# The SSD mixer's exit: gating, turning and projecting the scan's output in parts, with D x moved into the scan

## The reference, cut to what matters

```
    def finish(y_f, y_b, xs, z):
        bb, L = xs.shape[:2]
        y = y_f + flip(y_b) + D_skip[:, None] * xs
        y = y.reshape(bb, L, D_INNER).astype(z.dtype)
        return rmsnorm(y * jax.nn.silu(z), norm_w) @ out_w
```

```
        x = x + g1l * o_lat
            ctx = ctx + g1c * o_ctx
```

## Time and profile before

| | us |
|---|---|
| median of 3 runs | 4000.08 |
| lowest and highest | 3996.6, 4001.8 |
| the profiled execution's own time | 4008.97 |
| its span | 4007.2 |

### The profile page before, as it was taken

The page is one execution under the profiler, slowest core; times in us unless marked ns, Lnnn a source line. Parts: engine busy times, 40 slices in busy tenths (PEclk is TensorE's granted clock), DMA queues, the critical chain, the costliest instruction groups (busy, mean ns, idle before and its releaser), DMA issues. The chain is left out here.

```text
span 4007.2 us, 44450 instructions
## 1 busy us (share of the span) xinstructions
PE 3488.9 (87%) x17221; PEld 2512.8 (63%) x17225; DVE 2320.7 (58%) x2842; ACT 1673.2 (42%) x2522; POOL 1467.4 (37%) x706
## 2 busy tenths in 40 slices
PE   5999989967959999959897899997797997659997
PEld 3778878953447666646566455554685645538876
DVE  1037666772159999963663999997118842233311
ACT  3112123432028777751452677775323321342212
POOL 3323322340046666632004466664323201214432
PEclk9989998988969999979998899999878999779999
DMA  6324444432069999944104899997122223113130
GB/s 223 134 83 144 170 162 129 130 137 105 0 254 369 385 388 384 385 165 147 64 1 152 316 377 379 379 378 272 48 69 71 90 85 121 53 69 105 63 136 27
DMA packets 307214, 716.30 MB, mean 179 GB/s; under 512 B 16240, under 2 KB 63180, under 8 KB 303932
## 3 DMA queue, kind: packets, MB, share of 16 engines
q1 hardware_dynamic: 300176, 692.27, 46.6%
q0 software_dynamic: 6144, 20.98, 2.5%
q10 hardware_dynamic: 684, 0.21, 0.0%
HBM read 659.88 MB, written 53.54 MB: 178 GB/s over the span
## 5 line engine op out<-in xcount | busy, mean ns | idle before, releaser
L133 POOL TENSOR_TENSOR weights_low<-ring,weights_high 128x1024 fp32r<-128x1024 f32 (+2 forms) x210 | 497.0, 2372 | 1148.9 <-ACT weights_high L126 1141.4
L579 PE MATMUL ps<-h_parts,weights_high 128*128 128x512 f32 (+2 forms) x2528 | 744.4, 380 | 39.5 <-POOL weights_low L133 33.0
L579 PEld LDWEIGHTS ps<-h_parts,weights_high 128*128 128x128 f32 (+1 forms) x2528 | 465.0, 192 | 150.4 <-POOL weights_low L133 36.4
L579 PE MATMUL ps<-h_parts,weights_low 128*128 128x512 f32 (+2 forms) x1264 | 476.7, 377 | 0.0
L1741 DVE TENSOR_TENSOR more_low<-area,more_high 128x1024 fp32r<-128x1024 f32 x192 | 330.6, 1760 | 0.0
L1708 ACT ACTIVATE weights_high<-ring 128x1024 fp32r<-128x1024 f32 x256 | 271.2, 1061 | 137.2 <-PE ps L1641 92.6
L126 ACT ACTIVATE weights_high<-ring 128x1024 fp32r<-128x1024 f32 (+1 forms) x158 | 161.4, 1039 | 355.7 <-PE ps L579 231.7
L1708 ACT ACTIVATE more_high<-area 128x1024 fp32r<-128x1024 f32 x256 | 271.7, 1062 | 86.0 <-PE ps L1641 85.9
L1741 DVE TENSOR_TENSOR weights_low<-ring,weights_high 128x1024 fp32r<-128x1024 f32 x192 | 300.3, 1617 | 2.7 <-ACT weights_high L1708 2.7
L1612 POOL TENSOR_TENSOR more_low<-area,more_high 128x1024 fp32r<-128x1024 f32 x64 | 243.1, 3798 | 110.8 <-ACT more_high L1708 110.8
L579 PE MATMUL ps<-weights_high,h_parts 128*128 128x512 f32 (+2 forms) x832 | 256.0, 387 | 20.4 <-POOL weights_low L133 20.4
(11 more groups left out here) (433 smaller groups left out, 7244.4 us busy)
## 6 DMA issues: line engine op xcount, KB each, us to landing
ring<-in_moe_w SPq DMA_DIRECT2D x96, 2048.0 KB, 10.8
area<-in_moe_w SPq DMA_DIRECT2D x96, 2048.0 KB, 10.5
ring<-in_ada_w SPq DMA_DIRECT2D x24, 2048.0 KB, 8.0
ring<-in_ssd_in_w SPq DMA_DIRECT2D x12, 2048.0 KB, 11.1
ring<-in_w_in SPq DMA_DIRECT2D x11, 2048.0 KB, 8.0
ring<-in_w_ffn_in SPq DMA_DIRECT2D x10, 2048.0 KB, 7.7
area<-x_dram SPq DMA_DIRECT2D x18, 1024.0 KB, 5.0
ring<-in_ssd_out_w SPq DMA_DIRECT2D x4, 2048.0 KB, 7.9
```

The source lines that it names most:

```text
L133: pool.tensor_tensor(lo, views[k][:, ks, cols], hi, ALU.subtract).then_inc(self.low_p, 1)
L579: mm = pe.matmul(out, a, b, start=start and n == 0, stop=stop and n == 2)
```

## The change

- In the scan, GpSimd multiplies x by D for each head group of the first direction (into dx) and adds it to t.y when VectorE has written that. SyncE loads D ahead of the first chunk, and a chunk's buffers are free only when these additions are done too (skip_s).
- gate_turn takes the place of norm_turn. Tile by tile, from the last to the first, VectorE multiplies y by z, TensorE turns the product at once in four banks of four blocks, ScalarE squares and sums and writes each bank's high part, VectorE the low part. The root and its reciprocal are made once for all tiles at the end. Neither the root nor the norm weight is applied here.
- ssd_out takes the place of project_add. ScalarE and VectorE make the weights' high and low parts with the norm weight as a scale (one number for each row of out_w), TensorE makes three fp32r products, and VectorE takes the sums out of PSUM with the reciprocal root and the gate row in one instruction, and adds to X. GpSimd has no part in either stage.

```diff
--- before.py
+++ after.py
@@ -1005,6 +1005,8 @@
         state = st.sb("state", [P, DI])
         ex = st.sb("segment_exp", [P, 2, W4])
         acT, sel = st.sbr("acum_turned_parts", [P, NT, P]), st.sbr("pick_head_rows", [P, 2 * H])
+        dsk, dx = st.sb("d_skip", [P, H]), st.sb("d_times_x", [P, W])
+        d_in, skip_s = st.sem("d_in"), st.sem("skip_added")
         y1 = st.sb("y_off", [P, 2, W])
         y2 = st.sb("y_sum", [P, 2, W])
         acT_s, acT_h, acT_l = st.sem("acum_turned"), st.sem("acum_turned_high"), st.sem("acum_turned_low")
@@ -1022,11 +1024,13 @@
         @block.sync
         def _(sp):
             env.ring_.load_to(sp, len(env.ring_.ends) + SLOTS)
+            sp.dma_start(dsk, env.ins["ssd_D"].rearrange("a h -> (a h)").partition_broadcast(P)).then_inc(d_in, 16)
             v = lambda x, m: x[:, m % 2, :].rearrange("p (g c) -> p g c", g=G)
             for m, (d, i, c) in enumerate(steps):
                 if m >= 2:
 
                     sp.wait_ge(st_s, (m - 1) * G)
+                    sp.wait_ge(skip_s, min(m - 1, NT) * G)
                 tok = slice(c * P, (c + 1) * P)
                 sp.dma_start(xs[:, m % 2, :], env.x_dram[c, :, :]).then_inc(in_s[m % 2], 16)
                 sp.dma_start(v(bt, m), env.bt_dram[:, :, tok]).then_inc(in_s[m % 2], 16)
@@ -1142,13 +1146,22 @@
 
             scale_x(0, 0, G)
             scale_x(1, 0, G)
+            pool.wait_ge(d_in, 16)
             for m, (d, i, c) in enumerate(steps):
                 for g in range(G):
                     n = m * G + g
-                    if d == 1:
-
+                    yv = t.y[:, c, g * W:(g + 1) * W]
+                    if d == 0:
+                        pool.drain()
+                        pool.tensor_tensor(hv(dx), hv(xs[:, m % 2, g * W:(g + 1) * W]),
+                                           dsk[:, g * HPG:(g + 1) * HPG].unsqueeze(2).broadcast_to([P, HPG, HD]), ALU.mult)
+                        pool.drain()
                         pool.wait_ge(y2_s, n + 1)
-                        yv = t.y[:, c, g * W:(g + 1) * W]
+                        pool.tensor_tensor(yv, yv, dx, ALU.add).then_inc(skip_s, 1)
+                    else:
+                        pool.wait_ge(y2_s, n + 1)
                         pool.tensor_tensor(yv, yv, y2[:, n % 2, :], ALU.add).then_inc(yadd_s, 1)
 
                     if m >= 1 and m + 1 < len(steps) and 3 <= g < 7:
@@ -1325,6 +1338,159 @@
                     dve.scalar_tensor_tensor(o[:, j, :], o[:, j, :], ss[:, j:j + 1], spread[:, 0, :], ALU.mult, ALU.mult)
                     dve.drain()
                     dve.tensor_tensor(X[:, i, :], X[:, i, :], o[:, j, :], ALU.add)
+def gate_turn(env, base, y, rstd, parts):
+    ps, ring = env.ps, env.ring_
+    order = list(reversed(range(NT)))
+    with Stage(env, base) as st:
...
+        quad = lambda x, b: x[:, 4 * b:4 * b + 4, :].rearrange("p a b -> p (a b)")
+        bank = lambda p, b: ps[:, 4 * (p % 2) + b, :]
+        @block.sync
+        def _(sp):
+            for p, i in enumerate(order):
+                if p >= 2:
+                    sp.wait_ge(squared, p - 1)
+                sp.dma_start(zb[:, p % 2, :], env.z_dram[i, :, :]).then_inc(zt_in[p % 2], 16)
+            ring.load_to(sp, len(ring.ends) + SLOTS)
+        @block.vector
+        def _(dve):
+            def lows(p):
+                for b in range(4):
+                    dve.wait_ge(high, 4 * p + b + 1)
+                    hi, lo = (quad(x, b) for x in parts[order[p]])
+                    dve.tensor_tensor(lo, bank(p, b), hi, ALU.subtract).then_inc(low, 1)
+            for p, i in enumerate(order):
+                dve.wait_ge(zt_in[p % 2], 16 * (p // 2 + 1))
+                dve.tensor_tensor(y[:, i, :], y[:, i, :], zb[:, p % 2, :], ALU.mult).then_inc(gated, 1)
+                if p >= 1:
+                    lows(p - 1)
+            lows(NT - 1)
+            dve.wait_ge(squared, NT)
+            dve.tensor_scalar(rstd, rstd, EPS, None, ALU.add).then_inc(eps_in, 1)
+            dve.wait_ge(rooted, 1)
+            dve.reciprocal(rstd, rstd)
+        @block.scalar
+        def _(act):
+            for p, i in enumerate(order):
+                act.wait_ge(gated, p + 1)
+                act.drain()
+                act.activation(zb[:, p % 2, :], y[:, i, :], ACT.Square, scale=float(DI) ** -0.5,
+                               accum_out=rstd[:, i:i + 1]).then_inc(squared, 1)
+                for b in range(4):
+                    act.wait_ge(turned, 4 * p + b + 1)
+                    act.activation(quad(parts[i][0], b), bank(p, b), ACT.Copy).then_inc(high, 1)
+            act.wait_ge(eps_in, 1)
+            act.activation(rstd, rstd, ACT.Sqrt).then_inc(rooted, 1)
+        @block.tensor
+        def _(pe):
+            for p, i in enumerate(order):
+                pe.wait_ge(gated, p + 1)
+                for b in range(4):
+                    if p >= 2:
+                        pe.wait_ge(low, 4 * (p - 2) + b + 1)
+                    for k in range(4):
+                        a = (4 * b + k) * P
+                        tr = pe.transpose(bank(p, b)[:, k * P:(k + 1) * P], y[:, i, a:a + P], env.ident[:])
+                    tr.then_inc(turned, 1)
+def ssd_out(env, base, X, rstd, parts, gates, load):
+    ps, ring = env.ps, env.ring_
+    kd, pairs = 2 * KD, KD
+    per = pairs - 1 + NT
+    with Stage(env, base) as st:
...
+        cuts, m0, b0 = ring.take_cut([[(slice(k, k + 2), slice(0, HALF), NT if c == 1 and k == KD - 2 else 1)
+                                       for k in range(0, KD, 2)] for _ in range(2) for c in range(2)])
+        views = {cuts[0][0] + n: ring.view(cuts[0][0] + n, KD, HALF) for n in range(4)}
+        gain = lambda m, q: col(env, "ssd_norm_w", 2 * (m % pairs) + q)
+        h0 = ring.highs
+        ring.highs += len(cuts)
+        block = st.block()
+        @block.sync
+        def _(sp):
+            for u, r in enumerate(gates):
+                sp.dma_start(rows[:, u, :], r.partition_broadcast(P)).then_inc(rows_in, 16)
+            for i, src in load:
+                sp.dma_start(X[:, i, :], src).then_inc(x_in, 16)
+            ring.load_to(sp, len(ring.ends) + SLOTS)
+        @block.tensor
+        def _(pe):
+            for m, (_, ks, cols, _) in enumerate(cuts):
+                n, q = m // pairs, m % pairs
+                pe.wait_ge(ring.low_p, b0 + m + 1)
+                hi, lo = (ring.part(x, m, ks, cols) for x in (ring.hi, ring.lo))
+                for i in range(NT):
+                    if n == 1 and q == 0:
+                        pe.wait_ge(out, i + 1)
+                    for k in (2 * q, 2 * q + 1):
+                        mm = products(pe, ps[:, i, :], tuple(x[:, k, :] for x in parts[i]), (hi[:, k % 2, :], lo[:, k % 2, :]),
+                                      k == 0, k == kd - 1)
+                    if q == pairs - 1 or i == NT - 1:
+                        mm.then_inc(ring.done, 1)
+        @block.scalar
+        def _(act):
+            for m, (k, ks, cols, _) in enumerate(cuts):
+                if m == 0 or cuts[m - 1][0] != k:
+                    ring.wait(act, k)
+                if m >= CUTS:
+                    act.wait_ge(ring.done, cuts[m - CUTS][3])
+                hi = ring.part(ring.hi, m, ks, cols)
+                for q in range(2):
+                    mm = act.activation(hi[:, q, :], views[k][:, ks.start + q, :], ACT.Copy, scale=gain(m, q))
+                mm.then_inc(ring.high_s, 1)
+        @block.vector
+        def _(dve):
+            def low(m):
+                k, ks, cols, _ = cuts[m]
+                hi, lo = (ring.part(x, m, ks, cols) for x in (ring.hi, ring.lo))
+                dve.wait_ge(ring.high_s, h0 + m + 1)
+                for q in range(2):
+                    mm = dve.scalar_tensor_tensor(lo[:, q, :], views[k][:, ks.start + q, :], gain(m, q), hi[:, q, :],
+                                                  ALU.mult, ALU.subtract)
+                mm.then_inc(ring.low_p, 1)
+            def leave(n):
+                h = slice(n * HALF, (n + 1) * HALF)
+                for i in range(NT):
+                    dve.wait_ge(ring.done, m0 + n * per + pairs + i)
+                    dve.scalar_tensor_tensor(o[:, i % 2, :], ps[:, i, :], rstd[:, i:i + 1], rows[:, int(i >= NL), h],
+                                             ALU.mult, ALU.mult).then_inc(out, 1)
+                    dve.drain()
+                    dve.tensor_tensor(X[:, i, h], X[:, i, h], o[:, i % 2, :], ALU.add)
+            for m in range(pairs + CUTS - 1):
+                low(m)
+            dve.wait_ge(rows_in, 16 * len(gates))
+            dve.wait_ge(x_in, 16 * len(load))
+            leave(0)
+            for m in range(pairs + CUTS - 1, 2 * pairs):
+                low(m)
+            leave(1)
 
 
 def dispatch(env, layer, X, nt):
@@ -3142,12 +3308,12 @@
         ssd_project(env, t, b1)
         t.y = carve(env, base, [P, NT, DI])
         ssd_scan(env, t, base + NT * DI)
```

(10 more changed lines are left out.)

8 lines of the change are left out of this document (added).

## The result

The changed kernel takes 3930.86 us (median of four runs, 3927.69 to 3933.86); the ratio to the kernel before is 0.9816 with a 95% interval of 0.9804 to 0.9829. Off the 4000.08 us that I started from, that is 3926.5 us: 73.6 us gained (68.4 to 78.4), where I had forecast 64.0 with a range of 52 to 72. The profiled execution took 3933.86 us, its span 3932.1.

A forecast was written before the change was run, and what follows sets the result against it. TensorE bounds the scan and product, an exposed engine chain the norm stage between. -35.5 - 29.4 - 0.6 + 1.5 = -64.0 us, giving 3945.0 from the profiled 4008.97 or 3936 from the 4000.08 median; range 3928 to 3950 us.

The forecast's parts named there:

- Part 1: Norm stage becomes gate_turn: TensorE starts the product at 43.0 instead of 78.5 us, gain 35.5 us (29 to 38).
- exit: End of the product stage: ScalarE's copy between TensorE and VectorE falls out, gain 0.6 us.
- Part 2: Product stage: 576 fp32r matmuls at 0.2354 us replace 192 whole fp32 products, 165.0 to 135.6 us, gain 29.4 us.
- Part 3: Scan: an added small transfer and GpSimd's added product and addition per first-direction head group, loss 1.5 us.
- The small load: Scan start: one small SyncE transfer ahead of the first chunk's loads costs 0.4 us.
- the collisions: Scan: VectorE's form with both operands in SBUF waits for GpSimd's running instruction where GpSimd lags, 1.1 us.
- Rival 1: Scan: GpSimd's new product runs before VectorE's SBUF form in each group, costing 17 to 50 us; chance 0.09.
- Rival 2: gate_turn's engines do not overlap, 12.2 us a tile, leaving 2.5 us of the norm-stage gain, 3969 us; chance 0.04.
- Rival 3: Product stays at half clock: 564 further matmuls at 0.44 us cost 115 us, 4051 us in all; chance 0.02.

The follow-up runs named there:

- the profile with the delay: Changed kernel with five copies of 128x1024 on ScalarE added ahead of gate_turn's root; ratio to the kernel before 0.9837.
- D x twice: Changed kernel with GpSimd's product of D and x made twice in each of the 48 head groups; ratio to the kernel before 0.9879.

## Why the prediction came out as it did

- **Which step failed.** Two terms together; either alone would have left the time in the range. Part 1 was put at 35.5 us and measured 39.0. And all code behind the change stood in the sum at nothing, without a reason, where the attention stretch alone is 4 to 6 us shorter in both profiles of the changed kernel. The local parts gave 68 to 70 us, which is 3930 to 3932 us and in the range; the whole gave 73.6 (68.4 to 78.4). The attention's part is no sure gain of the change: it is gone again in the profile with the delay (372.4), and what decides it stays open. The sum also had 1.5 us of loss in the scan that the first pair of profiles does not show, and 30.0 us for product and exit where 29.2 came.
- **Part 1** (35.5 us, range 29 to 38): right in its steps, too small in size. It measured 39.0 (78.7 to 39.7), outside its own range. Up to tile 2 it ran as forecast (gated at 16.9 us against 17.0). Two terms were mis-sized. The pace of a tile was put at 5.2 us and measured 4.6: a subtraction shows 0.68 us, but the next one starts 0.60 after it (four take 2.48 together), where I had added a gap to each and put them 0.72 apart; over three tiles that is 1.8 us. The tail from tile 5's gating (902.1) to the reciprocal's end (908.0) took 5.9 us and not 7.4, mainly because 1.0 of the table load's 1.28 us ran before epsilon was in. From there to the first matmul are 3.1 us (3.0).
- **Part 2** (29.4): 29.2 with the exit. 576 matmuls are 136.1 us of busy time against 135.6 forecast, with a slow start, which the feed-forward product's 0.2354 had in it, too. I had put the two together at 30.0.
- **Exit** (0.6): not visible by itself; VectorE's two forms of 0.75 and 0.69 stand where I had them.
- **Part 3** (a loss of 1.5): the sum cannot be told from the scatter (in the first pair of profiles the scan as a whole has 272.8 twice, at a clock of 0.57 and 0.67 at its start), but its parts were wrong. The small load costs 1.8 (I had 0.4, from the issue alone), the collisions nothing that shows (I had 1.1).
- **The rule of the Trainium skill**, "SBUF — State Buffer", section "Who interferes with whom", that who issues first blocks the other: the case agrees for VectorE. Where VectorE is first, its form keeps 0.42 us; each of the slow instances, before and with D x twice, has a GpSimd instruction that began before it, and the mean with D x twice rises to 0.535. On table loads, the Trainium skill, "ScalarE: Activation LUTs", section "Table sets: the hidden batching unit", has about 2.7 us, which is not seen here: the load is 1.28 us again, the whole switch from the last copy's end to the root's start 1.3 (906.24 to 907.55), and less than 0.3 of it was on the path.
- **Rival 1** (17 to 50 us) did not come, and doubling the product did not bring it either: those 27 us are TensorE's waits for a scaling and its clock, not VectorE's form. Rival 2 did not come (4.6 us a tile, not 12.2). Rival 3 did not come: full clock 5 us after the start.

## What to carry to other kernels

In a stage that waits for a chain of engines, ask first which of its work can move under an engine that is full elsewhere: 31 of 39 us came from moving D x under the scan, 8 from the new pipeline. A cover that fits to 0.04 us is a gain, but price the next step, too: 0.76 us more in each of 48 groups cost 27, half of it as waits of TensorE and half as the lower clock around them. And give a range the scatter of all the code behind the change, when its TensorE work has gaps: a few us can come or go with nothing edited there. Before reading a stretch's length, compare its granted clock.

## What the runs showed of the hardware

One transfer of 16 KB to 128 partitions ahead of four loads of 2.5 MB in all delayed the matmuls that wait for them by 1.8 us, in all six profiles that had it there (first group at 16.9 to 17.2 us, against 15.1 to 15.4 in the seven without). A stretch of unchanged instructions took 365 to 372 us, by how much of TensorE's work fell on the lower clock, and the scan 253.4 to 258.3 us from its first group on, by the granted clock in its first 20 us (0.80 to 0.55). With D x twice, three waits of TensorE of 2.8 to 5.6 us in the scan each went with a fall to the lower clock.
